# The GpSimd sums of the adaptive modulation, moved to the first three feed-forward stages

## The chip, the cores and the metric

The kernel runs on 1 core of one Trainium2 chip. The metric is the time of one execution on the device in microseconds (us), smaller is better. The core has five engines that run their own instruction streams and meet at semaphores: TensorE (PE, matrix products, with its weight loads listed as PEld), VectorE (DVE), ScalarE (ACT), GpSimd (POOL) and SyncE (SP, which only starts transfers here). Tensors lie in the on-chip memory SBUF (128 partitions) or in the accumulation banks PSUM (`ps` in the program, 8 banks).

## What is computed

Three transformer blocks in a row, on 256 tokens of width 1024, all in fp32. The first two have feed-forward, mixer, feed-forward each; the third has the same shape, but its norms are modulated by a vector that is computed from a condition `c`:

```python
mod = (jax.nn.silu(c) @ w_ada[l] + b_ada[l]).reshape(b, N_SUB, 3, D_MODEL)   # 1024 -> 9216

def sublayer(h, i, fn, resid_w):
    shift, scale, gate = mod[:, i, 0, None, :], mod[:, i, 1, None, :], mod[:, i, 2, None, :]
    u = rms_norm(h, norm_pre[l, i]) * (1.0 + scale) + shift
    return h + resid_w * gate * rms_norm(fn(u), norm_post[l, i])
```

`c` is one row, so `silu(c) @ w_ada` is a product of a vector with a 1024 x 9216 matrix (37.7 MB). It depends on nothing that the first two blocks compute. `mod` is used from the fifth of the six feed-forward stages on.

## The kernel before

The program is a list of 13 stages, run one after the other: `ffn` (norm 0), `hg_in` (norm 1), `hg_out`, `ffn` (norm 2), `ffn` (norm 3), `fox_in` (norm 4), `fox_out`, `ffn` (norm 5), `ffn` (norm 6), `tm_in` (norm 7), `branch`, `tm_out`, `ffn` (norm 8). "The first, second, third feed-forward" below are norms 0, 2 and 3. All projections stream their weights through four slots of SBUF. SP loads a slot (`raw`), ScalarE rounds it (`w_hi`, L1181), VectorE subtracts to get the rest (`w_lo`, L1606, 128x2048), and TensorE multiplies three times for each product: L544, L545, L546. A feed-forward has 11 chunks; a projection has chunk pairs, of 48 products each chunk. Between two stages stand the residual (L1672), the square sum (L1212), the scaled row (L1640), the transposes on TensorE (L552) and the rounding of the transposed activations (L1195, L1621).

Each engine's order is the order of the code. The modulation has three pieces of 3072 columns. For each piece GpSimd runs 24 units of 128 columns: it starts a load of 512 KB from its own queue (L497) into one of two buffers, multiplies by `c_silu` (L505), adds halves three times (L508, L510, L512) and writes 128 columns of `ada_acc`. Two loads are ahead at any time. Then TensorE sums over the partitions in `ada_reduce` (L780: 24 products of 128 columns with one column of ones, each listed twice in the trace), and VectorE writes the modulation of the piece (`modulation`, L1658 to L1663). `ada_reduce` and `modulation` stand behind the second chunk of a stage: piece 0 in norm 3, piece 1 in norm 4 (`fox_in`), piece 2 in norm 6. There is one `ada_acc`, so GpSimd begins a piece when TensorE has reduced the one ahead (`ada_reduced`). It begins piece 0 when the activations of `hg_out` are transposed. Ahead of it GpSimd casts the masks `levels` (L489) and clears a buffer (L491), both for `hg_in`; between the first loads of piece 2 and its first unit it does two weight subtractions of `fox_in` (L479), and at the end eight more for later stages. `vectors()` on ScalarE makes `c_silu` in the first feed-forward.

All working buffers lie in one `arena`: `ada_acc` at 12288, the two load buffers behind it, `levels_raw` at 14336.

Of the kernel before, what the change touches and what calls it, by code (L numbers as in the profile page):

```python
# [25 lines left out]
P = 128  # L26
# [6 lines left out]
NF = F // FC  # L33
# [16 lines left out]
ADA_W = 3 * D  # L50
ADA_U = 128
# [10 lines left out]
LEVELS = (0, 1, 2, 4, 8, 16, 32, 64)  # L62
LEVEL_AT = (0,) + tuple(P + (P // 2) * n for n in range(len(LEVELS)))
HG_ORDER = (1, 0, 2, 3)


def shape_tables():
# [93 lines left out]
def build(nc, a, out):  # L161
# [4 lines left out]
    with ctx:  # L166
# [75 lines left out]
        modulated = region(4096, 2, 4 * P)  # L242
        gate_row = region(16384, D)
        rows_a, rows_b = region(8704, P), region(8832, P)
        ada_acc = region(12288, ADA_W)
        ada_raw = region(12288 + ADA_W, 2, KD, ADA_U)
        hg_v, hg_g = region(0, TILES, D), region(2048, TILES, D)
        hg_z, hg_qT, hg_sq = (region(4096, TILES, D) for _ in range(3))
# [2 lines left out]
        hg_f, hg_kT, hg_Q = region(8192, TILES, D), region(10240, TILES, D), region(12288, TILES, D)  # L251
        hg_sc = region(14336, TILES, HG_H, P)
        hg_sc_flat = region(14336, 2048)
        levels_raw = region(14336, LEVEL_AT[-1])
        levels = hidden.rearrange("p t f -> p (t f)")[:, 0:LEVEL_AT[-1] // 4].bitcast(U8)

        def hg_kept(c, t):
# [214 lines left out]
        @block.gpsimd  # L472
        def _(pool):
            step = InOrder(pool, pool_step)
            nc.gpsimd.memset(eps_col, EPS).then_inc(eps_ready, 1)
            def split_lo(s, n):

                pool.wait_ge(hi_ready[s], n + 1)
                nc.gpsimd.tensor_tensor(w_lo[:, s, :], raw[:, s, :], w_hi[:, s, :].bitcast(F32), ALU.subtract)\  # L479
                    .then_inc(lo_ready[s], 1)  # L480

            def split_gate_weights(st):
                for s in (2, 3):
                    split_lo(s, st.filled[s] + st.chunks // 2 - 1)


            pool.wait_ge(levels_loaded, 16)
            pool.wait_ge(hT_turned, NF + 1)
            nc.gpsimd.tensor_copy(levels, levels_raw).then_inc(levels_ready, 1)  # L489
            pool.wait_ge(levels_ready, 1)  # L490
            nc.gpsimd.memset(hg_sc_flat, 0.0).then_inc(hg_zeroed, 1)  # L491

            pool.wait_ge(turned, 4 * (by_name["hg_out"].turned + 1))
            pool.wait_ge(c_ready, 1)

            def ada_load(piece, u, s):
                nc.gpsimd.dma_start(ada_raw[:, s, :, :], w_ada[:, :, bass.ds(piece * ADA_W + u * ADA_U, ADA_U)])\  # L497
                    .then_inc(ada_loaded[s], 16)

            def ada_unit(piece, i, s):  # L500
                u = 2 * i + s
                n = piece * ADA_N + u
                r = ada_raw[:, s, :, :]
                pool.wait_ge(ada_loaded[s], 16 * (piece * (ADA_N // 2) + i + 1))
                nc.gpsimd.tensor_tensor(r, r, c_silu[:, :].unsqueeze(2).to_broadcast([P, KD, ADA_U]), ALU.mult)\  # L505
                    .then_inc(ada_scaled, 1)
                pool.wait_ge(ada_scaled, n + 1)
                nc.gpsimd.tensor_tensor(r[:, 0:4, :], r[:, 0:4, :], r[:, 4:8, :], ALU.add).then_inc(ada_by4, 1)  # L508
                pool.wait_ge(ada_by4, n + 1)
                nc.gpsimd.tensor_tensor(r[:, 0:2, :], r[:, 0:2, :], r[:, 2:4, :], ALU.add).then_inc(ada_by2, 1)  # L510
                pool.wait_ge(ada_by2, n + 1)
                nc.gpsimd.tensor_tensor(ada_acc[:, bass.ds(u * ADA_U, ADA_U)], r[:, 0, :], r[:, 1, :], ALU.add)\  # L512
                    .then_inc(ada_summed, 1)
                pool.wait_ge(ada_summed, n + 1)

            for piece in range(3):
                if piece:

                    pool.wait_ge(ada_reduced, piece)
                for s in range(2):  # L520
                    ada_load(piece, s, s)
                if piece == 2:
                    split_gate_weights(by_name["fox_in"])
                with pool.Fori(0, ADA_N // 2 - 1) as i:
                    for s in range(2):
                        ada_unit(piece, i, s)
                        ada_load(piece, 2 * i + 2 + s, s)
                for s in range(2):
                    ada_unit(piece, ADA_N // 2 - 1, s)

            pool.wait_ge(ada_reduced, 3)
            nc.gpsimd.dma_start(tm_bias.rearrange("p h n -> p (h n)"), a["da_bias"]).then_inc(bias_loaded, 16)
            split_gate_weights(by_name["tm_in"])
            for s in (0, 2, 1, 3):
                split_lo(s, by_name["branch"].filled[s])
            for s in (0, 1):
                split_lo(s, by_name["tm_out"].filled[s])
# [3 lines left out]
        def _(pe):  # L541
# [76 lines left out]
            def after_second_chunk(st):  # L618
                if st.norm >= 6:
                    pe.wait_ge(gate_row_ready, st.norm - 6 + 1)  # L620
                if st.norm in (3, 4, 6):
                    ada_reduce({3: 0, 4: 1, 6: 2}[st.norm])

            def ffn(st):
                filled, n = st.filled, st.ffn * NF
# [147 lines left out]

            def ada_reduce(piece):

                pe.wait_ge(ada_summed, ADA_N * (piece + 1))
                if piece:
                    pe.wait_ge(mod_ready, piece)
                for u in range(ADA_N):
                    last = nc.tensor.matmul(ps[:, SMALL_BANK, u:u + 1], ada_acc[:, u * P:(u + 1) * P],  # L780
                                            C["ones"][:, 0:1], start=True, stop=True)
                last.then_inc(ada_reduced, 1)

# [8 lines left out]
            def hgrn(st):  # L792
# [72 lines left out]

                first_chunk(st, [acc(0, t) for t in range(TILES)], proj0_done)
                chunk(st, 0, 1)
                chunk(st, 1, 0)
                pe.wait_ge(kept0, st.kept + 2)
                pe.wait_ge(kept1, st.kept + 2)  # L870
                turn(hg_z, 0)
                chunk(st, 1, 1)
                pe.wait_ge(kept0, st.kept + 4)
# [24 lines left out]
            def fox(st):  # L898

                wait_kept(st)  # L900
                pe.wait_ge(zf_split, 1)
                pe.wait_ge(mod_ready, 2)
                pe.wait_ge(small_loaded, 16 * 5)
                for t in range(TILES):
                    to = ps[:, SMALL_BANK, t * FOX_H:(t + 1) * FOX_H]
# [267 lines left out]
        def _(act):  # L1173
# [172 lines left out]
            def hgrn(st):  # L1346

                def weights(c):
                    for s in (2 * (c % 2), 2 * (c % 2) + 1):
                        split_hi(s, st.filled[s] + c // 2)  # L1350
# [18 lines left out]
                weights(3)  # L1369
                keep(2)  # L1370
                weights(4)
                for b in range(4):
                    t, at = b // 2, slice((b % 2) * COLS, (b % 2 + 1) * COLS)
                    act.wait_ge(hg_turned, b + 1)
                    nc.scalar.activation(hg_f[:, t, at], ps[:, 4 + b, :], ACT.Sigmoid).then_inc(hg_sig, 1)
                    nc.scalar.activation(hg_kT[:, t, at], ps[:, 4 + b, :], ACT.Sigmoid, scale=-1.0).then_inc(hg_k, 1)
# [177 lines left out]
            at = 48  # L1554
# [45 lines left out]
        def _(dve):  # L1600
# [51 lines left out]
            def modulation(st):  # L1652

                n = st.norm
                if n in (3, 4, 6):
                    piece = {3: 0, 4: 1, 6: 2}[n]
                    dve.wait_ge(ada_reduced, piece + 1)
                    step(nc.vector.tensor_tensor(modc[:, piece, :, :],  # L1658
                                                 ps[:, SMALL_BANK, 0:ADA_N].rearrange("p (m k) -> p m k", m=3),
# [120 lines left out]
            def hgrn(st):  # L1780
# [50 lines left out]
                keep(0)  # L1831
                weights(2)
                keep(1)
                weights(3)
                keep(2)
                weights(4)
# [341 lines left out]
```

## Time and profile before

| | us |
|---|---|
| median of 3 runs | 1827.97 |
| lowest, highest run | 1821.05, 1828.79 |
| the profiled execution's own time | 1828.06 |
| its span, from the first to the last instruction | 1826.4 |
| TensorE busy | 1713.1 |
| VectorE busy | 992.3 |
| ScalarE busy | 821.5 |
| GpSimd busy | 581.0 |
| mean granted TensorE clock | 0.952 |

A row of the timeline gives the start, the duration, the engine, the line and the operation with its tiles (`x48` is a group of 48 merged instructions), and in brackets how long the engine sat idle ahead of it and what ended that. Times are from the span's start. Products of TensorE overlap: a 128x512 product is listed with some 0.39 us and the next one starts 0.23 us behind it, so its pace is read from starts. A busy TensorE can be at either clock, and the granted clock of a stretch tells which.

### The profile page before, as it was taken

Reading aid. Unit: us, or ns where it says so; the run is one execution under the profiler, and the core shown is the slowest. Engines: PE = TensorE matmul, PEld = TensorE weight load, DVE = VectorE, ACT = ScalarE, POOL = GpSimd, SP = SyncE. Lnnn points to the kernel's source line nnn. Section 1 sums busy time; section 2 is a strip of 40 time slices with the busy share of each in tenths; the row PEclk is TensorE's granted clock in tenths of the full one; section 3 lists DMA queues with packets and bytes.
Section 4 is the critical chain, followed back from the end, with each engine's and each line's share of the span. In section 5 each row is a group of like instructions: output and inputs, shape, how many; then the busy total and the mean of one; then the engine's idle time right before and its main releaser. Section 6 shows DMA issues by size and latency. Waiting matters only on the chain.

```text
span 1826.4 us, 21892 instructions
## 1 busy us (share of the span) xinstructions
PE 1713.1 (94%) x7939; PEld 1421.0 (78%) x7939; DVE 992.3 (54%) x984; ACT 821.5 (45%) x966; POOL 581.0 (32%) x378
## 2 busy tenths in 40 slices
PE   6999999999999999979879999999997987789998
PEld 5888779878888888768767888788886875678886
DVE  4445668575655565643466645654456433565444
ACT  6565541454445344424344444544445455554343
POOL 0000000188885888852888900000000010500000
PEclk9999999999999999979878999999998997789999
DMA  6656453267784778645334765546563521425552
GB/s 215 204 186 212 147 192 110 91 218 243 243 263 147 255 238 260 228 157 189 93 117 159 231 197 185 178 147 193 186 214 119 208 92 47 138 92 185 186 185 88
DMA packets 208278, 321.35 MB, mean 176 GB/s; under 512 B 10920, under 2 KB 146402, under 8 KB 208226
## 3 DMA queue, kind: packets, MB, share of 16 engines
q1 hardware_dynamic: 195968, 281.05, 47.0%
q0 software_dynamic: 10512, 38.54, 6.8%
q10 hardware_dynamic: 1746, 1.05, 0.2%
q8 instruction: 35, 0.57, 0.1%
q14 instruction: 17, 0.14, 0.0%
HBM read 319.55 MB, written 1.05 MB: 176 GB/s over the span
## 4 chain that ended last, share of the span: by engine, by line
PE 74%; POOL 9%; DVE 7%; ACT 5%; issue 4%; DMA 1%; ACTq 0%; POOLq 0%; SPq 0%; DVEq 0%
PE ps L544 21%; PE ps L546 21%; PE ps L545 21%; POOL arena L508 3%; POOL arena L505 3%; DVE w_lo L1606 2%; POOL arena L510 2%; PE ps L590 1%; PE ps L842 1%; ACT w_hi L1181 1%; PE ps L780 1%; PE ps L648 1%; POOL arena L512 1%; PE ps L597 1%; PE ps L947 1%
## 5 line engine op out<-in xcount | busy, mean ns | idle before, releaser
L1606 DVE TENSOR_TENSOR w_lo<-raw,w_hi 128x2048 fp32r<-128x2048 f32 x256 | 630.7, 2472 | 326.1 <-ACT w_hi L1181 325.9
L544 PE MATMUL ps<-w_hi,actT_hi 128*128 128x512 f32 x1504 | 605.6, 403 | 21.1 <-DVE actT_lo L1634 7.8
L546 PE MATMUL ps<-w_hi,actT_lo 128*128 128x512 f32 x1504 | 594.5, 395 | 0.0
L545 PE MATMUL ps<-w_lo,actT_hi 128*128 128x512 f32 x1504 | 594.4, 395 | 0.0
L1181 ACT CAST w_hi<-raw 128x2048 fp32r<-128x2048 f32 x266 | 506.1, 1911 | 192.1 <-PE ps L546 190.4
L544 PEld LDWEIGHTS ps<-w_hi,actT_hi 128*128 128x128 f32 x1504 | 288.3, 192 | 82.5 <-DVE actT_lo L1634 8.5
L546 PEld LDWEIGHTS ps<-w_hi,actT_lo 128*128 128x128 f32 x1504 | 287.5, 191 | 62.5
L545 PEld LDWEIGHTS ps<-w_lo,actT_hi 128*128 128x128 f32 x1504 | 288.5, 192 | 57.7
L544 PE MATMUL ps<-w_hi,hT_hi 128*128 128x512 f32 x480 | 188.1, 392 | 2.6 <-DVE hT_lo L1731 2.6
L545 PE MATMUL ps<-w_lo,hT_hi 128*128 128x512 f32 x480 | 187.5, 391 | 0.0
L546 PE MATMUL ps<-w_hi,hT_lo 128*128 128x512 f32 x480 | 187.5, 391 | 0.0
L479 POOL TENSOR_TENSOR w_lo<-raw,w_hi 128x2048 fp32r<-128x2048 f32 x10 | 45.7, 4581 | 387.8 <-ACT w_hi L1181 387.8
L508 POOL TENSOR_TENSOR arena<-arena 128x512 f32<-128x512 f32 x72 | 151.2, 2100 | 5.6
L505 POOL TENSOR_TENSOR arena<-arena,c_silu 128x1024 f32<-128x1024 f32 x72 | 149.7, 2079 | 10.3 <-DMA arena<-w_ada_dram 7.9
L1278 ACT CAST hT_hi<-ps 128x512 fp32r<-128x512 f32 x60 | 35.2, 587 | 235.5 <-PE ps L648 235.5
L497 POOL DMA_DIRECT2D arena<-w_ada_dram x72 | 66.5, 924 | 227.1 <-PE ps L552 152.6
L544 PEld LDWEIGHTS ps<-w_hi,hT_hi 128*128 128x128 f32 x480 | 90.5, 188 | 21.7 <-DVE hT_lo L1731 3.0
L546 PEld LDWEIGHTS ps<-w_hi,hT_lo 128*128 128x128 f32 x480 | 90.5, 189 | 19.0
L545 PEld LDWEIGHTS ps<-w_lo,hT_hi 128*128 128x128 f32 x480 | 90.5, 189 | 18.7
L510 POOL TENSOR_TENSOR arena<-arena 128x256 f32<-128x256 f32 x72 | 102.3, 1420 | 5.6
L1731 DVE TENSOR_TENSOR hT_lo<-ps,hT_hi 128x512 fp32r<-128x512 f32 x60 | 41.4, 690 | 107.0 <-ACT hT_hi L1278 107.0
L1284 ACT ACTIVATE gate<-ps 128x256 f32<-128x256 f32 x66 | 25.3, 384 | 148.3 <-PE ps L546 130.3
(255 smaller groups left out, 1455.4 us busy)
## 6 DMA issues: line engine op xcount, KB each, us to landing
raw<-ffn_w_in_dram SPq DMA_DIRECT2D x176, 512.0 KB, 4.8
raw<-ffn_w_out_dram SPq DMA_DIRECT2D x88, 512.0 KB, 4.4
arena<-w_ada_dram POOLq DMA_DIRECT2D x72, 512.0 KB, 5.0
raw<-ffn_w_gate_dram SPq DMA_DIRECT2D x44, 512.0 KB, 3.9
raw<-ffn_w_up_dram SPq DMA_DIRECT2D x44, 512.0 KB, 4.9
raw<-ffn_w_down_dram SPq DMA_DIRECT2D x44, 512.0 KB, 4.5
raw<-w_in_dram SPq DMA_DIRECT2D x40, 512.0 KB, 4.5
raw<-hg_w_in_dram SPq DMA_DIRECT2D x32, 512.0 KB, 4.6
```

Of the source, the lines that this page charges most:

```text
L479: nc.gpsimd.tensor_tensor(w_lo[:, s, :], raw[:, s, :], w_hi[:, s, :].bitcast(F32), ALU.subtract)\
L497: nc.gpsimd.dma_start(ada_raw[:, s, :, :], w_ada[:, :, bass.ds(piece * ADA_W + u * ADA_U, ADA_U)])\
L505: nc.gpsimd.tensor_tensor(r, r, c_silu[:, :].unsqueeze(2).to_broadcast([P, KD, ADA_U]), ALU.mult)\
L508: nc.gpsimd.tensor_tensor(r[:, 0:4, :], r[:, 0:4, :], r[:, 4:8, :], ALU.add).then_inc(ada_by4, 1)
L510: nc.gpsimd.tensor_tensor(r[:, 0:2, :], r[:, 0:2, :], r[:, 2:4, :], ALU.add).then_inc(ada_by2, 1)
L544: nc.tensor.matmul(to, hi, whi, start=start, stop=False, skip_group_check=True)
L545: nc.tensor.matmul(to, hi, wlo, start=False, stop=False, skip_group_check=True)
L546: return nc.tensor.matmul(to, lo, whi, start=False, stop=stop, skip_group_check=True)
L1181: nc.scalar.copy(w_hi[:, s, :], raw[:, s, :]).then_inc(hi_ready[s], 1)
L1278: nc.scalar.copy(hT_hi[:, :, :], ps[:, HT_BANK, :].rearrange("p (f t) -> p f t", f=2)).then_inc(hT_hi_ready, 1)
L1606: nc.vector.tensor_tensor(w_lo[:, s, :], raw[:, s, :], w_hi[:, s, :].bitcast(F32), ALU.subtract)\
L1731: nc.vector.tensor_tensor(hT_lo[:, :, :], ps[:, HT_BANK, :].rearrange("p (f t) -> p f t", f=2), hT_hi[:, :, :].bitcast(F32), ALU.subtract) ...
```

## The change

GpSimd sums piece 0 at the very start, as soon as `c_silu` is there, in the first feed-forward, then casts the masks and clears the buffer. Pieces 1 and 2 follow each other without a wait once the activations of `hg_out` are transposed, since piece 2 has a buffer of its own (arena 8192; the masks' raw form moves to 10240). The two subtractions for `fox_in` come behind piece 2. `ada_reduce` and `modulation` move from norms 3, 4 and 6 to norms 1 (`hg_in`), 3 and 4, again behind the second chunk. Three waits are new: TensorE waits for `mod_ready` ahead of the transposes of `hg_in`, ScalarE for `levels_ready` ahead of its sigmoids there, and GpSimd for `ada_reduced` ahead of the clearing.

```diff
+ADA_AT = {1: 0, 3: 1, 4: 2}
...
-        ada_acc = region(12288, ADA_W)
+        ada_acc = [region(at, ADA_W) for at in (12288, 12288, 8192)]
...
-        levels_raw = region(14336, LEVEL_AT[-1])
+        levels_raw = region(10240, LEVEL_AT[-1])
...
-            for piece in range(3):
-                if piece:
-
-                    pool.wait_ge(ada_reduced, piece)
+            def ada_piece(piece):
                 for s in range(2):
                     ada_load(piece, s, s)
-                if piece == 2:
-                    split_gate_weights(by_name["fox_in"])
                 with pool.Fori(0, ADA_N // 2 - 1) as i:
...
+            pool.wait_ge(c_ready, 1)
+            ada_piece(0)
+            pool.wait_ge(levels_loaded, 16)
+            pool.wait_ge(hT_turned, NF + 1)
+            nc.gpsimd.tensor_copy(levels, levels_raw).then_inc(levels_ready, 1)
+            pool.wait_ge(ada_reduced, 1)
+            nc.gpsimd.memset(hg_sc_flat, 0.0).then_inc(hg_zeroed, 1)
+            pool.wait_ge(turned, 4 * (by_name["hg_out"].turned + 1))
+            ada_piece(1)
+            ada_piece(2)
+            split_gate_weights(by_name["fox_in"])
...
-                if st.norm in (3, 4, 6):
-                    ada_reduce({3: 0, 4: 1, 6: 2}[st.norm])
+                if st.norm in ADA_AT:
+                    ada_reduce(ADA_AT[st.norm])
...
                 chunk(st, 0, 1)
+                after_second_chunk(st)
                 chunk(st, 1, 0)
                 pe.wait_ge(kept0, st.kept + 2)
                 pe.wait_ge(kept1, st.kept + 2)
+                pe.wait_ge(mod_ready, 1)
                 turn(hg_z, 0)
...
                 weights(2)
                 keep(1)
+                modulation(st)
                 weights(3)
```

GpSimd from its start, before: the cast and the clearing (L489, L491), then the loads of the first piece.

```order
L475 MEMSET small 128x1
L489 CAST hidden<-arena 128x576
L491 MEMSET arena 128x2048
L497 DMA arena<-w_ada_dram 128x8x128 x2
```

After, the same place: the loads and the units of piece 0, its last unit, and then the cast and the clearing.

```order
L476 MEMSET small 128x1
L489 DMA arena<-w_ada_dram 128x8x128 x2
...
L504 TENSOR_TENSOR arena<-arena 128x128
L522 CAST hidden<-arena 128x576
L524 MEMSET arena 128x2048
L489 DMA arena<-w_ada_dram 128x8x128 x2
```

What moved: a whole piece of 24 units now stands ahead of the cast and the clearing that `hg_in` needs.

TensorE in `hg_in`, between its second and third chunk, before: the products follow each other.

```order
L544 MATMUL ps<-w_hi,actT_hi 128x512
L545 MATMUL ps<-w_lo,actT_hi 128x512
L546 MATMUL ps<-w_hi,actT_lo 128x512
L544 MATMUL ps<-w_hi,actT_hi 128x512
L545 MATMUL ps<-w_lo,actT_hi 128x512
```

After, the same place (the three products are L542 to L544 in its numbering):

```order
L542 MATMUL ps<-w_hi,actT_hi 128x512
L543 MATMUL ps<-w_lo,actT_hi 128x512
L544 MATMUL ps<-w_hi,actT_lo 128x512
L780 MATMUL ps<-consts_sb,arena 128x1 x24
L542 MATMUL ps<-w_hi,actT_hi 128x512
```

What moved: 24 one-column products, which wait for GpSimd, stand here now. The same row left the feed-forward of norm 6; nothing else on TensorE, VectorE (the three small instructions of `modulation` go with it) or ScalarE changed its place.

## Rows read from the trace of the kernel before

**Rows 1.** The page's first part: busy time of each engine.

```profile
PE 1713.1 (94%) x7939; PEld 1421.0 (78%) x7939; DVE 992.3 (54%) x984; ACT 821.5 (45%) x966; POOL 581.0 (32%) x378
```

**Rows 2.** Engines by stretch: feed-forwards of norms 0, 2, 6, and the fox stage.

```profile
core 0: us, PE busy (x) PEld busy (x) DVE busy (x) ACT busy (x) POOL busy (x), PEclk, DMA share, GB/s
34.00:204.00 170.00, 167.43 (x752) 137.84 (x752) 85.78 (x75) 97.61 (x88) 3.61 (x2) 0.99 0.60 193
...
386.00:559.00 173.00, 173.00 (x785) 143.02 (x784) 102.10 (x68) 74.80 (x67) 152.24 (x97) 1.00 0.76 243
...
870.00:990.00 120.00, 100.98 (x487) 87.32 (x488) 71.44 (x72) 47.31 (x109) 101.91 (x84) 0.80 0.33 102
...
1190.00:1375.00 185.00, 185.00 (x856) 154.20 (x856) 90.90 (x76) 77.75 (x73) 0.60 (x1) 0.98 0.57 184
```

**Rows 3.** Timeline around the reduction of piece 1 in fox_in.

```profile
790.80 0.93 POOL L497 DMA_DIRECT2D arena<-w_ada_dram  x1 [0.66 <-POOL arena L512]
...
791.96 0.39 PE L546 MATMUL ps<-w_hi,actT_lo 128*128 128x512 f32 x1
...
802.49 0.45 POOL L512 TENSOR_TENSOR arena<-arena 128x128 f32<-128x128 f32 x1
...
803.00 10.40 PE L780 MATMUL ps<-consts_sb,arena 128*128 128x1 f32 x48 [10.65 <-POOL arena L512]
...
813.26 0.77 PE L544 MATMUL ps<-w_hi,actT_hi 128*128 128x512 f32 x1
```

**Rows 4.** Timelines of TensorE and GpSimd around the reduction of piece 0, norm 3.

```profile
570.51 2.44 POOL L512 TENSOR_TENSOR arena<-arena 128x128 f32<-128x128 f32 x1
590.45 1.80 POOL L497 DMA_DIRECT2D arena<-w_ada_dram  x2 [17.50 <-PE ps L780]
...
583.36 6.51 PE L780 MATMUL ps<-consts_sb,arena 128*128 128x1 f32 x48
589.73 1.09 PE L648 MATMUL ps<-consts_sb,hidden 128*128 128x128 f32 x4
590.48 0.78 PE L544 MATMUL ps<-w_hi,actT_hi 128*128 128x512 f32 x1
...
594.38 0.39 PE L544 MATMUL ps<-w_hi,actT_hi 128*128 128x512 f32 x1
```

**Rows 5.** Timeline around the reduction of piece 2, norm 6.

```profile
1200.81 6.18 PE L780 MATMUL ps<-consts_sb,arena 128*128 128x1 f32 x48
...
1206.85 1.09 PE L648 MATMUL ps<-consts_sb,hidden 128*128 128x128 f32 x4
```

**Rows 6.** Timeline: when `c_silu` is there, and when GpSimd starts piece 0.

```profile
34.08 0.21 ACT L1538 ACTIVATE c_silu<-cols 128x8 f32<-128x8 f32 x1 [2.96 <-DVE lb L2115]
...
356.78 1.95 POOL L497 DMA_DIRECT2D arena<-w_ada_dram  x2 [152.57 <-PE ps L552]
```

**Rows 7.** TensorE's second transposes at the start of hg_in and of fox_in.

```profile
217.28 1.03 PE L552 MATMUL ps<-consts_sb,arena 128*128 128x128 f32 x8
...
772.69 1.03 PE L552 MATMUL ps<-consts_sb,arena 128*128 128x128 f32 x8
```

**Rows 8.** L1606 by stretch (ns min/median/max; 34 to 204, 386 to 559), VectorE and waits in fox.

```profile
L1606 DVE TENSOR_TENSOR w_lo<-raw,w_hi x30: 2280/2293/2295, 40.9 to 199.5; 128x2048 fp32r<-128x2048 f32 x30
...
L1606 DVE TENSOR_TENSOR w_lo<-raw,w_hi x31: 2291/2486/4241, 391.3 to 554.2; 128x2048 fp32r<-128x2048 f32 x31
...
886.37 7.28 DVE L1934 TENSOR_TENSOR arena<-arena,small 128x2048 f32<-128x2048 f32 x2
...
917.47 0.17 DVE L1958 TENSOR_SCALAR small<-small 128x8 f32<-128x8 f32 x1
...
928.90 1.64 DVE L1958 TENSOR_SCALAR small<-small 128x8 f32<-128x8 f32 x1
...
957.87 3.82 DVE L1606 TENSOR_TENSOR w_lo<-raw,w_hi 128x2048 fp32r<-128x2048 f32 x1
...
PE ps L928 <- DVE arena L1934: 4.2, 2, 2.9
```

More of the change, by code:

```diff
@@ L484, in split_gate_weights @@
                     split_lo(s, st.filled[s] + st.chunks // 2 - 1)
[L487 to L494, printed above, removed]
             def ada_load(piece, u, s):
@@ L511, in ada_unit @@
                 pool.wait_ge(ada_by2, n + 1)
-                nc.gpsimd.tensor_tensor(ada_acc[:, bass.ds(u * ADA_U, ADA_U)], r[:, 0, :], r[:, 1, :], ALU.add)\
+                nc.gpsimd.tensor_tensor(ada_acc[piece][:, bass.ds(u * ADA_U, ADA_U)], r[:, 0, :], r[:, 1, :], ALU.add)\
                     .then_inc(ada_summed, 1)
                 pool.wait_ge(ada_summed, n + 1)
-            for piece in range(3):
-                if piece:
-                    pool.wait_ge(ada_reduced, piece)
+            def ada_piece(piece):
                 for s in range(2):
                     ada_load(piece, s, s)
-                if piece == 2:
-                    split_gate_weights(by_name["fox_in"])
                 with pool.Fori(0, ADA_N // 2 - 1) as i:
@@ L774, in ada_reduce @@
             def ada_reduce(piece):
+                if piece == 0:
+                    pe.wait_ge(consts_loaded, 16)
                 pe.wait_ge(ada_summed, ADA_N * (piece + 1))
@@ L779, in ada_reduce @@
                 for u in range(ADA_N):
-                    last = nc.tensor.matmul(ps[:, SMALL_BANK, u:u + 1], ada_acc[:, u * P:(u + 1) * P],
+                    last = nc.tensor.matmul(ps[:, SMALL_BANK, u:u + 1], ada_acc[piece][:, u * P:(u + 1) * P],
                                             C["ones"][:, 0:1], start=True, stop=True)
@@ L901, in fox @@
                 pe.wait_ge(zf_split, 1)
-                pe.wait_ge(mod_ready, 2)
+                pe.wait_ge(mod_ready, 3)
                 pe.wait_ge(small_loaded, 16 * 5)
@@ L1371, in hgrn @@
                 weights(4)
+                act.wait_ge(levels_ready, 1)
                 for b in range(4):
@@ L1654, in modulation @@
                 n = st.norm
-                if n in (3, 4, 6):
-                    piece = {3: 0, 4: 1, 6: 2}[n]
+                if n in ADA_AT:
+                    piece = ADA_AT[n]
                     dve.wait_ge(ada_reduced, piece + 1)
```

## The prediction

> **What bounds the kernel now.** I read the page's busy times first: TensorE works 1713.1 us of 1826.4 [rows 1], so what counts is what keeps TensorE waiting or slow. Then the busy times by stretch [rows 2]. In the feed-forwards TensorE is busy all the time at full clock, also in the one of norm 2, where GpSimd sums a piece beside it (173.00 of 173.00 us, GpSimd 152.24 busy, 243 GB/s moved). The fox stage is another matter: 100.98 of 120 us busy at a mean clock of 0.80, so there TensorE waits for others, and it does so in small pieces. Last come the three places where the modulation meets TensorE, since the chain that ended last runs on GpSimd for 9% of the span. That share isn't 9% to be won. Only the wait at its end costs anything.
>
> That wait is in fox_in [rows 3]. TensorE's last product of the second chunk starts at 791.96; the next would start 0.23 us later, at 792.2. It starts its reduction at 803.00 instead, when GpSimd's last unit ends (802.49 + 0.45). So 10.8 us are lost. The 24 one-column products then take until 813.26, that is 10.3 us, where the same 24 took 6.4 us (583.36 to 589.73) when TensorE came to them without a wait [rows 4]. The difference of 3.9 us is the clock: at rest TensorE fell to the lower of its two levels (1.2 GHz). One more thing costs time at each reduction. The one-column products leave TensorE at the lower clock even without a wait: behind them nine products take 3.90 us (590.48 to 594.38) where at 0.23 us each they would take 2.0. That is 1.9 us. A reduction on time costs 6.4 + 1.9 = 8.3 us, one that waited costs its wait and 10.3 + 1.9 = 12.2 us.
>
> **Part 1: piece 0 goes to the first feed-forward, its reduction to hg_in.** GpSimd starts when `c_silu` is there, 34.08 + 0.21 = 34.3 us, and some 0.1 us for the semaphore: 34.4 [rows 6]. How long does a piece take? Piece 0 took from 356.78 to 570.51 + 2.44 = 572.95, so 216.2 us [rows 4, 6]; piece 1 from 590.45 to 802.94, so 212.5 us [rows 3, 4]. Both lay beside a feed-forward with the same three subtractions L1606 a chunk that piece 0 will meet now. So GpSimd ends between 246.9 and 250.6; I take the middle, 248.8. When does TensorE want it? In hg_in the second transposes start at 217.28, in fox_in at 772.69 [rows 7], and from there to the point of the reduction the same 78 products run: 792.2 - 772.7 = 19.5 us. In hg_in that gives 236.8. GpSimd is 10.1 to 13.8 us late, 11.9 in the middle. If its work slows the stage change ahead of it by a few us, that is covered by the same wait, as TensorE then only comes later to a point at which it waits anyway. So the whole cost of part 1 is 11.9 + 12.2 = **24.1 us lost**. The wait of fox_in is not gone; it has moved.
>
> Who stands behind these waits? VectorE stops in `modulation` until the reduction is over, and its subtractions for the fourth chunk stand behind it. TensorE first does the third chunk, 48 products at 0.23 us or some 11 us, for which the weights are ready, and the two subtractions take 2 x 2.29 [rows 8], so they are hidden. The cast of the masks comes at 248.8 and 2 us more; ScalarE's sigmoids need TensorE's third chunk and the transposes, over 20 us later. Both are priced at nothing; if that cover went, the cast would cost its 2 us. The clearing of the buffer (under 2 us) is likewise due only after all of that.
>
> **Part 2: pieces 1 and 2 without a gap; reductions in norm 3 and fox_in.** Piece 1 starts by the same signal as piece 0 did and ends as that did, at 572.95 on the old clock, 10.4 us ahead of the reduction at 583.36 [rows 4]. Same cost as before: 0. Piece 2 starts at once instead of at 590.45. With 212.5 to 216.2 us it ends at 785.5 to 789.2, and TensorE comes at 792.2. It is on time by 3.0 to 6.7 us. Then fox_in pays 8.3 us instead of 10.8 + 12.2 = 23.0: **14.7 us won**. GpSimd's units now also run between 573 and 590 beside the start of the third feed-forward; the same pair of engines cost TensorE nothing in norm 2 [rows 2], so 0, with 1 us as the upper end. The two subtractions for fox_in are behind piece 2 and start as before when ScalarE has rounded their weights.
>
> **Part 3: no GpSimd beside the fox stage.** In the fox stretch GpSimd was 101.91 of 120 us busy with piece 2 [rows 2]; now it rests. In fox VectorE is waited for, and GpSimd makes it slow. L1606 takes 2.28 to 2.30 us with GpSimd at rest and up to 4.24 us beside it [rows 8]. On TensorE's path I find three such places: L1934, two of 128x2048 in 7.28 us where two quiet L1606 of that size take 4.6, so 2.7 (TensorE stood 4.2 us before L928 for it); L1958, 1.64 against 0.17, so 1.5; the L1606 at 957.87, 3.82 against 2.29, so 1.5. Sum **5.7 us won**. The lower end is 0, if ScalarE or the transposes are late next; the upper end is 9, with the other lengthened instructions, which I take as off the path.
>
> **Part 4: norm 6 loses its reduction.** 1200.81 to 1206.85 is 6.0 us [rows 5], and 1.9 for the clock as above: **7.9 us won**. That stage is TensorE's alone (185.00 of 185.00 us [rows 2]), so nothing else comes up.
>
> **A rule against the change.** L1606 was up to 1.95 us longer beside GpSimd, yet TensorE lost nothing in that feed-forward [rows 2, 8], so I charge the first feed-forward nothing beside the wait. The Trainium skill, "SBUF — State Buffer", section "SBUF: two separate sides", says that a VectorE operation with two SBUF inputs and a GpSimd operation that reads SBUF hold one port pair exclusively, and the loser stands still for the whole instruction. By that rule all 30 subtractions of the first feed-forward could be late; were all of it on the path, 30 x 1.95 would be an estimate of 58 us lost. The trace agrees with the lock, but not with that price: in norm 2 the delays are inside VectorE's idle time.
>
> **The sum.** 24.1 - 14.7 - 5.7 - 7.9 = -4.2 us. The profiled execution took 1828.06 us, which is 0.1 from the median of 1827.97: 1823.9 us, say 1824.
>
> **The rivals.** *More won (about 1815).* GpSimd ends at the early end (1.9 less wait), the clock doesn't fall in the shorter wait of hg_in (3.9 less), and fox gives its 9 us (3.3 more): 9.1 us more, 1814.8. For it: TensorE comes to hg_in's reduction 2 to 3 us later than 236.8 if GpSimd slows the stage change, so it rests less. Against it: in fox_in it did fall.
>
> *Piece 2 is late again (about 1830).* The margin of 3.0 to 6.7 us is small beside one unit of 9 us. If it is used up, TensorE rests for 1 to 4 us and the reduction is slow (3.9): 5 to 8 us less won, 1829 to 1832. For it: in piece 1 the last units ran beside a VectorE that stood still in `modulation`; they won't now.
>
> *Slower than before (about 1840).* The first feed-forward is the one stage where GpSimd has not been seen, and ScalarE has more to do there, 97.61 of 170 us against 74.80 of 173 [rows 2]. If that shifts VectorE's subtractions so that they meet more of GpSimd's additions, the piece takes longer, and every microsecond is paid by TensorE in hg_in. This decides from 227 us on for the piece (9.5 us a unit instead of 9.0): at 13 us more wait the total is 0.5% above before. At 232 us, 16 more, the time is 1840. Against it: two pieces at two places agree within 4 us.
>
> **How the numbers follow.** Forecast 0.56, more won 0.20, late again 0.17, slower 0.07. The range takes the forecast's own ends (2 us for the piece, 6 for fox) and reaches to both neighbours: 1812 to 1834. A measurement of this kernel can tell about 0.5% (9 us) from no change. Faster by more than that needs under 1818.8: most of the second case and a little of the first, 0.26. Slower by more: 0.08. Within: 0.66.
>
> **What would show it.** In the profile after: GpSimd's first load at 34.4 and its last unit of piece 0 at 247 to 251; L780 in hg_in behind an idle time of 8 to 14 us, 10.3 us long; L780 in the third feed-forward and in fox_in without a wait, 6.4 us long; none in norm 6; L1934's pair near 4.6 us. The forecast is wrong if TensorE shows idle time inside the first feed-forward, if a piece takes over 225 us, or if fox's stretch is no shorter with its VectorE instructions short.

## The result and the profile after

Each run stands beside runs of the kernel before on the same chip; a ratio is taken against those.

| kernel | median us | lowest to highest | ratio to before [95%] | profiled execution: span, clock |
|---|---|---|---|---|
| before | 1827.5 | 1819.0 to 1833.7 | | 1826.4, 0.952 |
| changed | 1832.0 | 1828.7 to 1835.8 | 1.0029 [1.0016, 1.0041] | 1827.8, 0.951 |

The change costs some 5 us where the prediction had 4 us won, so its sign was wrong. 1832.0 lies within 1812 to 1834 and within 0.5% of before. Two more measurements gave 1.0022 and 1.0032 (below). The kernel before scatters by 15 us and the changed one by 7, so one trace of each is not enough: the two profiled spans here differ by 1.4 us only. I therefore read three traces of the changed kernel and two of the one before, stage by stage.

First the places that the prediction named. The page's busy times of the changed kernel, against [rows 1]:

```profile
PE 1715.5 (94%) x7939; PEld 1421.8 (78%) x7939; DVE 1005.4 (55%) x984; ACT 821.9 (45%) x966; POOL 615.4 (34%) x378
```

GpSimd has the same 378 instructions, yet is busy 34.4 us longer, and VectorE 13.1 us. The work is the same, so the two meet more often: GpSimd's addition of 128x512 takes 2306 ns in the mean instead of 2100, where it takes 1.26 to 1.30 us with VectorE at rest. TensorE's busy time is the same within 2.4 us.

Timeline of the changed kernel around the reduction in `hg_in`; start, duration, engine, then the idle time before it and its releaser in brackets:

```profile
33.60 1.95 POOL L489 DMA_DIRECT2D arena<-w_ada_dram  x2 [32.63 <-ACT c_silu L1541]
...
247.90 0.45 POOL L504 TENSOR_TENSOR arena<-arena 128x128 f32<-128x128 f32 x1
248.42 0.66 POOL L522 CAST hidden<-arena 128x576 uint8<-128x576 f32 x1
...
248.50 10.37 PE L780 MATMUL ps<-consts_sb,arena 128*128 128x1 f32 x48 [13.08 <-POOL arena L504]
...
258.94 1.80 POOL L524 MEMSET arena<- 128x2048 f32 x1 [9.86 <-PE ps L780]
```

This answers to [rows 3], whose 10.65 us of waiting and 10.40 us of reduction it repeats at an earlier place. In the second trace of the kernel before the wait was longer, 15.01 us. GpSimd ended at 248.35 (predicted 248.8); TensorE was there at 235.4 and stood 13.08 us.

The reduction in `fox_in`, in the changed kernel's third trace:

```profile
818.36 0.46 POOL L504 TENSOR_TENSOR arena<-arena 128x128 f32<-128x128 f32 x1
818.87 7.99 PE L780 MATMUL ps<-consts_sb,arena 128*128 128x1 f32 x48 [1.85 <-POOL arena L504]
```

Piece 2 is just in time, or 1.85 us late; the margin of 3.0 to 6.7 us is not there. In the first trace its last unit ended at 817.9 and the reduction began at 818.49 without a wait, in the second at 818.4 and 818.88.

The stages in all traces, in us between the same landmarks on TensorE: the first transposes of a stage (L552 before, L550 after), for "to reduction" the start of L780, for "fox_in" to "fox" the products of L928 (L930 after), and for the last two the products of L1006 (L1008 after). The feed-forwards are numbered in their order, so norm 5 is the fourth and norm 6 the fifth; these two stand under their norms. The last column is the span.

| trace | to hg_in | hg_in | hg_out, 2nd ffn | 3rd ffn to reduction | on to fox_in | fox_in | fox | fox_out, norm 5 | norm 6 | norm 7's stage | rest | span |
|---|---|---|---|---|---|---|---|---|---|---|---|---|
| before | 208.4 | 139.3 | 215.3 | 20.4 | 177.4 | 132.9 | 70.3 | 214.2 | 201.7 | 103.1 | 343.4 | 1826.4 |
| again_before | 206.3 | 140.9 | 215.4 | 20.7 | 178.2 | 131.1 | 76.8 | 216.7 | 203.3 | 101.6 | 338.3 | 1829.3 |
| changed | 206.4 | 164.7 | 217.0 | 23.5 | 177.4 | 114.5 | 71.9 | 214.3 | 193.2 | 104.1 | 341.0 | 1827.8 |
| again_after | 206.8 | 164.9 | 216.8 | 21.9 | 179.0 | 114.4 | 75.2 | 214.5 | 193.2 | 104.2 | 341.1 | 1831.9 |
| after_3 | 206.7 | 167.3 | 215.6 | 20.1 | 177.8 | 116.2 | 75.2 | 214.5 | 193.2 | 104.1 | 341.1 | 1831.9 |
| mean changed less mean before | -0.7 | +25.6 | +1.1 | +1.3 | +0.2 | -17.0 | +0.5 | -1.0 | -9.3 | +1.8 | +0.2 | +2.7 |

The last row is the account of the change. The two large gains and the large loss are what was predicted; they leave -0.7 us, and the small terms decide the sign. Its sum of 2.7 us is less than the 4 to 6 us of the three ratios: the quickest executions of the kernel before, near 1819, are in no trace, and in which stage they win is open.

### The profile page after: what moved, and what is told of

Read it like the earlier page. It is cut to its first block, busy times and chain, and to the rows that moved or that the text cites. A ratio compares the mean times of both kernels' runs of the same rounds, so it can differ in the third digit from the quotient of the medians.

```text
span 1827.8 us, 21892 instructions
## 1 busy us (share of the span) xinstructions
PE 1715.5 (94%) x7939; PEld 1421.8 (78%) x7939; DVE 1005.4 (55%) x984; ACT 821.9 (45%) x966; POOL 615.4 (34%) x378
## 4 chain that ended last, share of the span: by engine, by line
PE 74%; POOL 9%; DVE 7%; ACT 5%; issue 3%; DMA 1%; ACTq 0%; POOLq 0%; SPq 0%; DVEq 0%
PE ps L542 21%; PE ps L543 21%; PE ps L544 21%; POOL arena L497 3%; POOL arena L500 3%; DVE w_lo L1609 2%; POOL arena L502 2%; PE ps L588 1%; PE ps L842 1%; PE ps L780 1%; POOL arena L504 1%; ACT w_hi L1183 1%; PE ps L646 1%; PE ps L595 1%; PE ps L949 1%
## 5 line engine op out<-in xcount | busy, mean ns | idle before, releaser
L1609 DVE TENSOR_TENSOR w_lo<-raw,w_hi 128x2048 fp32r<-128x2048 f32 x256 | 650.6, 2550 | 320.3 <-ACT w_hi L1183 320.2
L542 PE MATMUL ps<-w_hi,actT_hi 128*128 128x512 f32 x1504 | 606.5, 403 | 20.1 <-DVE actT_lo L1637 7.8
L544 PE MATMUL ps<-w_hi,actT_lo 128*128 128x512 f32 x1504 | 595.8, 396 | 0.0
L542 PEld LDWEIGHTS ps<-w_hi,actT_hi 128*128 128x128 f32 x1504 | 289.1, 192 | 82.6 <-DVE actT_lo L1637 8.5
L544 PEld LDWEIGHTS ps<-w_hi,actT_lo 128*128 128x128 f32 x1504 | 288.6, 192 | 62.5
L542 PE MATMUL ps<-w_hi,hT_hi 128*128 128x512 f32 x480 | 187.4, 390 | 1.0 <-DVE hT_lo L1734 1.0
L544 PE MATMUL ps<-w_hi,hT_lo 128*128 128x512 f32 x480 | 186.9, 389 | 0.0
L500 POOL TENSOR_TENSOR arena<-arena 128x512 f32<-128x512 f32 x72 | 166.0, 2306 | 5.6
L489 POOL DMA_DIRECT2D arena<-w_ada_dram x72 | 66.5, 924 | 199.6 <-PE ps L550 119.4
L502 POOL TENSOR_TENSOR arena<-arena 128x256 f32<-128x256 f32 x72 | 115.4, 1603 | 5.6
L542 PEld LDWEIGHTS ps<-w_hi,hT_hi 128*128 128x128 f32 x480 | 90.1, 188 | 20.0 <-DVE hT_lo L1734 1.4
L544 PEld LDWEIGHTS ps<-w_hi,hT_lo 128*128 128x128 f32 x480 | 90.1, 188 | 18.8
L543 PEld LDWEIGHTS ps<-w_lo,hT_hi 128*128 128x128 f32 x480 | 90.1, 188 | 18.6
```

The costliest lines, as they stand in the source:

```text
L542: nc.tensor.matmul(to, hi, whi, start=start, stop=False, skip_group_check=True)
L543: nc.tensor.matmul(to, hi, wlo, start=False, stop=False, skip_group_check=True)
L544: return nc.tensor.matmul(to, lo, whi, start=False, stop=stop, skip_group_check=True)
L1609: nc.vector.tensor_tensor(w_lo[:, s, :], raw[:, s, :], w_hi[:, s, :].bitcast(F32), ALU.subtract)\
```

## The experiments

**Both kernels again.** No edit; the same two programs.

> The kernel before, unchanged, against itself: ratio 1.000 within its interval. Its trace is a second one of the same program. If what GpSimd and VectorE cost each other at a stage change is a matter of how they happen to meet, the distance from the first transposes (L552) of the third feed-forward to its reduction (20.35 us in the first trace) and the fox stage (890.5 to 978 there) differ by 1 to 3 us between the two traces; if it is fixed by the program, they agree within 0.5 us.

> The changed kernel once more: ratio 1.001 to 1.004. Theory A (chance meetings at the stage changes): a second trace again has L780 in hg_in behind an idle time of 12 to 14 us, but other lengths at the start of the third feed-forward (first transposes to reduction, 23.5 us in the first trace against 20.35 before). Theory B (GpSimd without a gap always costs there): 23 us or more again.

> The changed kernel once more, as the base of the three runs beside it: 4 to 5 us above the kernel before, ratio 1.0025, as the two measurements so far (1.0029 and 1.0022). The rival is the prediction's, 4.2 us below; that would need both to have been chance.

Measured: again_before 1827.8 us, 0.9998 [0.9980, 1.0017]; again_after 1832.2 us, 1.0022 [1.0003, 1.0042]; after_3 1834.0 us beside before's 1826.4, 1.0032 [1.0007, 1.0056]. The change is a loss, three times in three. Its traces gave the table above, and with it the size of what varies from one execution of the same program to the next: `fox` 70.3 or 76.8 us, the third feed-forward's start 20.1 to 23.5, the rest 338 to 343. The start's 23.5, 21.9 and 20.1 us are of one and the same program, so the first theory holds: how GpSimd and VectorE happen to meet there, and no fixed price.

**The gap put back in front of piece 2.**

```diff
             ada_piece(1)
+            pool.wait_ge(ada_reduced, 2)
             ada_piece(2)
```

> The changed kernel, but GpSimd begins piece 2 only when TensorE has reduced piece 1, as it waited before. This takes GpSimd away from the start of the third feed-forward. Theory B: that start is 3 us shorter than in the changed kernel (20.4 us again), and fox_in gets back its wait of some 11 us and the slow reduction, so about 10 us more than the changed kernel in sum, 1840 to 1843. Rival (GpSimd there costs nothing, the 3 us were chance): 13 us more, 1845.

Measured: 1845.5 us, 1.0088 [1.0063, 1.0114], 13 us above the changed kernel. Timeline of gap in `fox_in`:

```profile
828.13 10.40 PE L781 MATMUL ps<-consts_sb,arena 128*128 128x1 f32 x48 [10.69 <-POOL arena L504]
```

The wait and the slow reduction of [rows 3] are back, and `fox_in` takes 127.6 us instead of 115.0. So the third buffer is worth its 13 us, near the 14.7 of the prediction's part 2. The expectation's rival (1845) came, not its theory B: the third feed-forward's start took 20.1 us here, as it did in after_3 without this wait. The loss lies elsewhere.

**The reduction of `hg_in` later.** `ada_reduce(0)`, the wait for it and VectorE's `modulation` move behind the fourth chunk and the forget gate's work, so that GpSimd has ended before TensorE asks.

```diff
                 chunk(st, 0, 1)
-                after_second_chunk(st)
...
-                pe.wait_ge(mod_ready, 1)
...
+                ada_reduce(0)
+                pe.wait_ge(mod_ready, 1)
```

> The changed kernel with the reduction of piece 0 in hg_in two chunks later (ahead of the second transposes there), where GpSimd has long ended. If the wait in hg_in is what the change costs, it goes: 13 us of idle time, and the reduction takes 6 to 8 us instead of 10.4, so 13 to 17 us less than the changed kernel, 1815 to 1819, and less than before too. Rival (GpSimd's work beside the first feed-forward costs it as well, and TensorE only waits elsewhere afterwards): under 6 us less.

> The run late once more, beside the changed kernel on one chip. By stages of the traces it wins hg_in's 6 to 7 us alone (from 164.7 to 165.7 down to 159.0 us between the first transposes of hg_in and of hg_out): 6 to 7 us below the changed kernel, which is 2 us below the kernel before. Rival, from its first run (0.9971 of the kernel before) : 5 us below the kernel before.

Measured: 1824.8 us both times; 0.9971 [0.9954, 0.9989] and 0.9996 [0.9971, 1.0021]; 7.4 and 9.2 us less than the changed kernel beside it. `hg_in` falls from 165.6 to 159.0 and 157.7 us. That is 7 to 8 of the 15 to 17.5 us that `hg_in` gains when the reduction is on time (free_first and no_sums, below). Timeline of late there:

```profile
255.78 2.39 POOL L504 TENSOR_TENSOR arena<-arena 128x128 f32<-128x128 f32 x1
258.23 0.66 POOL L522 CAST hidden<-arena 128x576 uint8<-128x576 f32 x1
258.93 0.60 ACT L1378 ACTIVATE arena<-ps 128x512 f32<-128x512 f32 x1 [3.91 <-POOL hidden L522]
...
269.24 10.37 PE L780 MATMUL ps<-consts_sb,arena 128*128 128x1 f32 x48 [4.91 <-issue]
```

The wait for GpSimd is gone from TensorE, but ScalarE's sigmoid now stands behind the cast of the masks (3.91 us <- L522), and TensorE still comes to its 24 products after some rest and does them at 1.2 GHz in 10.37 us. The first expectation (13 to 17 us) counted the wait and the slow reduction both as gone. The piece itself also ended 8 to 10 us later (258.2 instead of 248.4), as TensorE and VectorE now worked on beside it.

**The first piece without its sums.** Left out: the loads and three of the four instructions of each unit of piece 0; one addition of 128 cleared columns a unit remains. The other pieces are whole.

```diff
+                if piece:
                     pool.wait_ge(ada_loaded[s], ...)
                     nc.gpsimd.tensor_tensor(r, r, c_silu...)
```

> The changed kernel with the sums of the first piece alone left out: none of its loads, and one short GpSimd addition of cleared columns per unit; the second and third piece are as in the changed kernel. It gives the price of the first piece. From the traces: hg_in's first transposes to hg_out's took 164.7, 164.9 and 165.7 us with the first piece's sums before it and 148.1 without any sums. Theory that the whole difference is the wait, the slow reduction behind it and the clock: 16 to 18 us below the changed kernel, near 1813. Rival: part of the 148.1 came from the other pieces' absence, or the start of the span (206 to 209 us whichever kernel) gives part of it back: 10 to 12 us below.

Measured: 1815.4 us, 0.9932 [0.9910, 0.9954], 18.6 us below after_3 beside it. `hg_in` took 150.7 us instead of 165.6 to 167.3. Timeline of free_first in `hg_in`:

```profile
234.73 7.20 PE L785 MATMUL ps<-consts_sb,arena 128*128 128x1 f32 x48
```

TensorE comes to the place at 234.7, as it did with GpSimd beside it (235.4), and without a wait needs 7.20 us. So the first piece costs 13.1 us for the wait and 3.2 for 10.37 against 7.20, 16.3 together, where the medians differ by 18.6. `hg_in` is 14.9 us shorter than in the mean of the changed kernel's traces. The two intervals put together leave 12 to 24 us, so the rival's 10 to 12 are just outside: neither the other pieces nor the start of the span (206.4 us here, 206.4 to 206.8 in the changed kernel) accounts for a part of it.

**No sums at all.** Left out: the loads and sums of all three pieces, as above.

> The changed kernel, with the modulation's sums left out: no loads of w_ada, and in place of a unit's four GpSimd instructions one short addition of cleared columns, with the same signals, so that the reductions stand where they stood and nothing waits for them. What it gives is the whole price of GpSimd's work. Theory: the wait of 13.0 us in hg_in and the reduction's 10.3 us instead of 6.4, and 3 to 5 us where VectorE is slowed elsewhere: 20 to 22 us below the changed kernel, so near 1811. Rival: the clock gives most of the wait back (TensorE, rested for 13 us, is throttled less later): 8 to 12 us below the changed kernel, near 1822.

Measured: 1802.8 us, 0.9884 [0.9857, 0.9911] beside before's 1824.2. The changed kernel did not run beside it; at its three ratios (1.0022 to 1.0032) it would be at 1828.2 to 1830.0 there, so GpSimd's work and what waits for it cost 25 to 27 us, give or take 5 by the interval. I had expected 20 to 22, which is not excluded; the rival's 8 to 12 is. The loads are left out with the sums, and what each of the two costs was not measured apart. By stages against the changed kernel's means: `hg_in` 148.1 (17.5 less), `hg_out` and the second feed-forward 213.8 (2.7 less), the third's start 19.4 (2.4 less), on to `fox_in` 175.6 (2.5 less), `fox` 66.0 (8.1 less), the rest 337.6 (3.5 less). These add up to more than the medians differ by, as this trace (span 1793.3) is the quickest execution of the six, and `fox` and the rest have no GpSimd sums beside them in either kernel, so their 8.1 and 3.5 are scatter of the kind that the next experiment shows. The first feed-forward loses next to nothing to GpSimd (to `hg_in` 206.4 to 206.8 us with it, 206.4 in free_first and 205.8 here without), as the prediction said. The second, and the third in all, are 2.7 and 4.9 us shorter here, in one trace; that suggests a price there which a TensorE "busy all the time" doesn't show. Part of it is in places like this one, in the changed kernel at the start of the third feed-forward:

```profile
586.52 4.81 DVE L1609 TENSOR_TENSOR w_lo<-raw,w_hi 128x2048 fp32r<-128x2048 f32 x1
587.26 1.91 POOL L497 TENSOR_TENSOR arena<-arena,c_silu 128x1024 f32<-128x1024 f32 x1
589.25 3.23 POOL L500 TENSOR_TENSOR arena<-arena 128x512 f32<-128x512 f32 x1
...
592.45 1.11 DVE L1624 SCALAR_TENSOR_TENSOR actT_lo<-ps,cols,actT_hi 128x128 fp32r<-128x128 f32 x4
...
593.62 1.21 PE L595 MATMUL ps<-w_hi,actT_lo 128*128 128x512 f32 x4 [1.63 <-DVE actT_lo L1624]
...
594.27 2.06 DVE L1643 TENSOR_SCALAR arena<-x,small 128x1024 f32<-128x1024 f32 x1
```

And the same place in gap, where the two engines happen to miss each other:

```profile
589.15 2.28 DVE L1610 TENSOR_TENSOR w_lo<-raw,w_hi 128x2048 fp32r<-128x2048 f32 x1
...
592.55 1.11 DVE L1625 SCALAR_TENSOR_TENSOR actT_lo<-ps,cols,actT_hi 128x128 fp32r<-128x128 f32 x4
...
594.38 0.75 DVE L1644 TENSOR_SCALAR arena<-x,small 128x1024 f32<-128x1024 f32 x1
```

The subtraction of 128x2048 took 4.81 us against 2.28, and the scaling 2.06 against 0.75; behind them TensorE waited 1.63 us for `actT_lo` and then ran at 1.2 GHz for a while (its products start 0.43 us apart instead of 0.23, up to 598). The stretch took 23.5 us there and 20.1 in gap; after_3 took 20.1 too, with GpSimd as busy. In the kernel before, GpSimd had already ended piece 0 some 10 us ahead of this reduction, and the stretch took 20.4 and 20.7. The Trainium skill ("SBUF — State Buffer", "SBUF: two separate sides") speaks of a lock for a whole instruction; the rows above agree with it. GpSimd's multiplication took its usual 1.91 us up to 589.17, and the subtraction beside it ended 2.16 us later, at 591.33, about the 2.28 that it takes alone. The addition that GpSimd began at 589.25 ended at 592.48, 1.15 us behind the subtraction, where it takes 1.29 in gap. So each stood while the other worked, and VectorE lost 2.5 us and GpSimd 1.9. Why the subtraction, listed from 586.52 on, did not come ahead of the multiplication of 587.26, the rows don't show.

**Fox without GpSimd, in the kernel before.** Piece 2 of the kernel before starts only once `fox_out`'s activations are turned.

```diff
+                if piece == 2:
+                    split_gate_weights(by_name["fox_in"])
+                    pool.wait_ge(turned, 4 * by_name["fox_out"].turned + 1)
                 for s in range(2):
                     ada_load(piece, s, s)
```

> The kernel before, with one thing moved: GpSimd starts the third piece's loads and sums only once the four chunks of fox_out are turned, so that the whole attention stage between fox_in and fox_out has no GpSimd beside it. The prediction gave that stage 5.7 us of relief (the long VectorE operations of L1934, L1958 and L1606). If it is right: 4 to 6 us faster than the kernel before, ratio about 0.9975. Rival: the two traces of the kernel before show that stretch 70.3 and 76.8 us long, the two of the changed kernel 71.9 and 75.2, so the stage does not care for GpSimd (its TensorE runs at 1.2 GHz there and the waits fill with that): ratio 1.000, within 1 us. The third piece then ends near 1182, before its reduction at 1200.

Measured: 1827.0 us beside 1824.2, 1.0004 [0.9986, 1.0022]: nothing won, and 5.7 us (0.9969) are excluded for the run as a whole. The edit doesn't take GpSimd's work away, though. Piece 2 now runs from 965.4 to 1177.5, beside `fox_out` and all of norm 5's feed-forward, and that stretch took 216.5 us where it took 214.3 to 214.9 in traces with no sums there. So some 2 us of a gain may be hidden, and `fox` itself must be read from its own stretch. The stretches of `fox` by busy times (stretch, its length, then TensorE, its weight loads, VectorE, ScalarE and GpSimd busy, the granted clock, DMA share, GB/s); before first, then again_before, before_fox_quiet, changed, after_3 and late_2:

```profile
893.70:963.95 70.25, 56.02 (x296) 50.74 (x296) 39.69 (x45) 28.16 (x78) 59.38 (x51) 0.74 0.34 105
```

```profile
892.54:969.38 76.84, 62.95 (x296) 56.67 (x296) 36.61 (x45) 28.19 (x78) 64.66 (x58) 0.62 0.34 103
```

```profile
889.50:963.90 74.40, 62.73 (x295) 55.50 (x295) 33.93 (x45) 28.16 (x78) 0.00 (x0) 0.64 0.10 29
```

```profile
903.35:975.21 71.86, 59.25 (x295) 53.01 (x296) 34.08 (x45) 28.16 (x78) 0.00 (x0) 0.69 0.10 30
```

```profile
903.80:979.00 75.20, 63.47 (x296) 56.84 (x296) 34.09 (x45) 28.16 (x78) 0.00 (x0) 0.66 0.09 29
```

```profile
901.35:970.63 69.28, 55.60 (x296) 49.64 (x296) 33.99 (x45) 28.16 (x78) 0.00 (x0) 0.75 0.10 31
```

VectorE is quicker without GpSimd (34 us busy against 37 to 40), and TensorE's idle time falls a little: 14.2 and 13.9 us with GpSimd, 11.7, 12.6, 11.7 and 13.7 without. But the length follows the clock. At a granted 0.74 the same 296 matmuls take 56.0 us, at 0.62 they take 63.0. At like clock the stretch is 1 to 2.4 us shorter without GpSimd (69.3 at 0.75 against 70.25 at 0.74; 74.4 at 0.64 against 76.8 at 0.62). That is less than the 3.0 us of the prediction, and small beside these 7, which fall either way: the twelve traces without GpSimd there lie at 66.0 to 75.2 us, 72.9 in the mean, and the two with it at 70.3 and 76.8.

**The third reduction in the feed-forward of norm 5.** The expectations call this the fifth feed-forward; it is the fourth. late, with norm 5 in place of norm 4 for piece 2 and buffers exchanged to fit; then the same with GpSimd waiting ahead of piece 2 until TensorE has reduced piece 1.

```diff
-ADA_AT = {1: 0, 3: 1, 4: 2}
+ADA_AT = {1: 0, 3: 1, 5: 2}
...
             ada_piece(1)
+            pool.wait_ge(ada_reduced, 2)
             ada_piece(2)
```

> The run named late, with the third reduction moved from fox_in on to the stage after fox_out (fifth feed-forward), where TensorE has full rate. In the traces of the changed kernel the reduction in fox_in took 8.06 us and the one at full rate 6.2. Theory that the time lies in where a reduction stands: 1.9 us less than late, so 7 us less than the kernel before (ratio 0.9960). Rival: only TensorE's total of work counts and the clock gives it back: as late, ratio 0.9971.

> late5, where GpSimd waits between its second and third piece until TensorE has reduced the second (near 611 us instead of 600 us), with its third piece then ending near 829 us, in fox_in, and read only after fox_out. Theory that GpSimd beside the start of the third feed-forward costs (there the stretch between first transposes and reduction was 20.4 and 20.7 us in the kernel before, 23.5, 21.9, 22.0 in the changed one and late): 1 to 2 us less than late5. Rival, from the run gap, whose stretch was 20.1 with GpSimd just as busy there: chance from trace to trace, so nothing is won, and GpSimd's extra 11 us in fox_in slow VectorE there: 0 to 2 us more than late5.

> The run late5_gap once more. Its stages: hg_in 158.2, fox_in without its reduction 104.0 instead of 114.5, fox_out with it 221.8 instead of 214.4: by these 6.6 + 10.5 - 7.4 = 9.7 us below the changed kernel, so 5 to 6 below the kernel before, ratio 0.997. Rival: its first measurement, 0.9963, was lucky beside late5's 0.9997 (the two traces differ by 1.2 us), and the two together, 0.998, are what it is: 3.5 us below the kernel before.

Measured: late5 (without the wait) 1824.2 us, 0.9997 [0.9977, 1.0017]; late5_gap 1818.8 us, 0.9963 [0.9944, 0.9983]; late5_gap_2 1815.4 us beside before's 1826.4, 0.9934 [0.9912, 0.9957], and 18.6 us below the changed kernel beside it. late5's own expectation failed on both sides: neither 0.9960 nor the rival's 0.9971 is within its interval. late5_gap_2 came out lower than the 0.997 that its stages gave. Timeline of late5_gap_2 at the moved reduction:

```profile
1007.41 5.41 PE L781 MATMUL ps<-consts_sb,arena 128*128 128x1 f32 x48
```

It takes 5.41 us there, and 7.99 us in after_3's `fox_in`. `fox_in` without it took 103.9 us (115.0 with it), `fox_out` and norm 5's feed-forward 221.8 (214.4): 3.7 us won, of which the duration is 2.6. The stages in the traces of the experiments:

| trace | to hg_in | hg_in | hg_out, 2nd ffn | 3rd ffn to reduction | on to fox_in | fox_in | fox | fox_out, norm 5 | norm 6 | norm 7's stage | rest | span |
|---|---|---|---|---|---|---|---|---|---|---|---|---|
| gap | 209.3 | 165.7 | 215.6 | 20.1 | 177.2 | 127.6 | 75.1 | 214.5 | 193.2 | 104.2 | 341.1 | 1843.7 |
| late | 209.5 | 159.0 | 216.9 | 21.9 | 177.9 | 116.6 | 74.7 | 214.9 | 193.2 | 104.4 | 337.8 | 1826.7 |
| late_2 | 209.5 | 157.7 | 216.9 | 20.1 | 177.8 | 119.5 | 69.2 | 214.6 | 193.2 | 104.2 | 341.0 | 1823.7 |
| late5 | 209.6 | 157.7 | 216.5 | 21.8 | 177.2 | 105.4 | 72.0 | 221.7 | 193.1 | 104.3 | 337.9 | 1817.2 |
| late5_gap | 206.8 | 158.3 | 216.8 | 21.9 | 178.8 | 104.0 | 74.7 | 221.8 | 193.2 | 104.3 | 337.9 | 1818.4 |
| late5_gap_2 | 206.7 | 158.4 | 216.7 | 22.0 | 178.9 | 103.9 | 74.7 | 221.8 | 193.2 | 104.3 | 337.9 | 1818.4 |
| before_fox_quiet | 206.1 | 138.1 | 215.7 | 20.6 | 178.8 | 130.1 | 74.4 | 216.5 | 201.7 | 104.7 | 338.3 | 1825.1 |
| free_first | 206.4 | 150.7 | 215.5 | 20.6 | 177.9 | 116.0 | 71.9 | 214.3 | 193.2 | 104.1 | 341.0 | 1811.6 |
| no_sums | 205.8 | 148.1 | 213.8 | 19.4 | 175.6 | 114.8 | 66.0 | 214.7 | 193.2 | 104.2 | 337.6 | 1793.3 |

The wait that late5_gap adds didn't do what its theory said. The third feed-forward's start is 21.9 with it and 21.8 without, since piece 1 still runs there; its other effects cancel in the traces (1818.4 against 1817.2). Yet the median of twelve is 5.4 us lower than late5's. Half of late5's executions lie at 1825.8 to 1828.6 and half at 1816.8 to 1822.6, while late5_gap's are spread from 1808.9 to 1825.6. Why, no trace shows; that stays open. What is shown is that late5_gap beats both kernels: its ratios to the kernel before are 0.9963 and 0.9934, with medians 5 and 11 us lower.

## Why the prediction was wrong

Sum predicted -4.2 us, found by the table +2.7 (by the three ratios +4 to +6). The step that failed is the relief of the `fox` stage in part 3: 3.0 us for L1958 and L1606 that the stretch did not give. It is the largest single miss. The other misses are small terms that stood at nothing, and a part stays open. Term by term:

- **The first feed-forward, 0.** Right: -0.7, with GpSimd 146 us busy beside it.
- **hg_in, +24.1.** Right in mechanism and nearly in size: +25.6. The wait was 13.1 instead of 11.9 us, since TensorE came at 235.4, not 236.8; GpSimd's end was 0.4 us off. The reduction took 10.4 us as forecast. free_first shows this loss by itself.
- **fox_in, -14.7, with L1934's -2.7.** Right: -17.0 together. L1934's part came: its pair took 4.5 us, and TensorE's wait ahead of L928 fell from 4.2 and 3.4 us in the two traces before to 1.7. But the step "it is on time by 3.0 to 6.7 us" failed. Pieces 1 and 2 took 437.8 us from 380.15 on, not 428.7 to 432.4, and the margin was under 0.6 us or a wait of 1.85. The rival of a late piece 2 named the mechanism; of its 5 to 8 us only 1.4 to 3.5 came, no wait or 1.85 us, and a reduction of 7.8 to 8.1 us rather than 6.4, with a granted clock of 0.64 to 0.68 in 818 to 828. That the measured 1832 lies at this rival's 1829 to 1832 is therefore chance.
- **fox, the other -3.0 (L1958 and L1606).** This step failed: +0.5, from two traces before that differ by 6.5. The VectorE instructions did get short, as the prediction's last paragraph asked for (L1958's place 0.17 us, the subtractions 2.29), with the stretch no shorter, which it had named as the sign that it is wrong. before_fox_quiet, with GpSimd's work moved out of the stretch, took 74.4 us in it and won nothing as a whole. The prediction added up VectorE's shortened instructions as if each were TensorE's time. At like clock 1 to 2.4 us of it came. What the rows of one trace could not tell is that the stretch takes 70 or 77 us in the same program, by how long TensorE gets 2.4 GHz in it.
- **The start of the third feed-forward, 0 with 1 as the upper end.** Nearly right: +1.3 in the mean of three traces, up to 3.1 in one. The ten traces of the changed kernel and its variants with sums there have 21.4 us in the mean, the two of the kernel before and before_fox_quiet's 20.6, so the difference is 0.8. The reason given ("the same pair of engines cost TensorE nothing in norm 2") did take a steady stretch for a stage's start. At the start TensorE waits for VectorE's next result, and the rows above show how that costs 3 us in one trace; in others the same program pays nothing.
- **`hg_out` and the second feed-forward, no term.** +1.1, and the cause is open: GpSimd stands beside this stretch in both kernels and starts 9.1 us behind its first transposes in both. The three traces have 217.0, 216.8 and 215.6 us, the last as in the kernel before.
- **norm 6, -7.9.** Right, -9.3.
- **Norm 7's stage, +1.8.** Not in the sum, and nothing of the change stands there. The granted clock of the stretch was 0.95 and 0.97 before and 0.93 after, so norm 6's removed reduction might be paid back in part. The eight traces of the experiments without that reduction lie at 104.1 to 104.4 too, but before_fox_quiet, which has it, is at 104.7 with a clock of 0.93. So this is more likely chance of before's two traces.

Between forecast and table lie 6.9 us: 3.5 in `fox`, 1.5 in `hg_in`, 2.4 in the two stretches around the second and third feed-forward's start, 1.8 in norm 7's stage; the rest is -2.3. The 1 to 3 us more that the ratios show are in no trace and stay open. The forecast's "4 us faster" came from subtracting 28 us of gains from 24 of loss, and the miss of one 3 us term together with two smaller ones was enough to turn its sign.

## What to carry over

When a sum is a few us between gains and losses of 25, look at the cheap terms first, and take a second trace: `fox` alone differed by 6.5 us between two traces of one program, more than the whole forecast. A price of nothing for one engine beside another should come from the same kind of place, a stage's start from a stage's start. Time won on VectorE in a stage where TensorE waits in small pieces is not TensorE's time one for one. And a reduction that must wait for a slow engine belongs where its operand is long there: this one took 5.4 us in norm 5's feed-forward, some 8 in `fox_in` and 10.4 behind a long wait.

## What the runs showed of the hardware

The same 24 one-column products took 5.41 us at a granted clock of 1.00 (in norm 5's feed-forward, three traces), 10.37 to 10.40 at 0.50, and values between at clocks between. Without a wait ahead of them they took 5.7 to 8.3 us in the third feed-forward and norm 6, 7.2 and 7.6 in `hg_in`, and 7.4 to 8.1 in `fox_in`, although the granted clock was 1.00 in the 10 us ahead of each; why norm 5's place is the quick one is open. Behind rests of TensorE of 4.7 to 15 us they took the full 10.4, behind two of 1.8 us 8.0 and 10.1. One VectorE subtraction of 2.28 us was stretched to 4.81 by GpSimd beside it. And GpSimd's loads and sums cost 25 to 27 us in all, give or take 5, of which 16.3 are the 13.1 us of waiting in `hg_in` and the slower reduction behind it.
